# A routed-expert decoder layer: output products by column halves, eleven places for expert weights

## The chip, the core and the metric

The kernel runs on one core of a Trainium2 chip. The core has a matrix engine (TensorE, PE in the rows), VectorE (DVE), ScalarE (ACT), GpSimd (POOL) and SyncE (SP), which run their own streams of instructions and meet by semaphores, and 16 DMA engines, which serve the queues that SP and POOL write. The metric is the device time of one execution in microseconds (us).

## What is computed

One decoder layer on 544 token rows of 1024 values in float32: 512 prompt rows (token tiles 0 to 3 of 128) and 32 decode rows (tile 4). After the attention and pooling branches comes the part that the change touches, cut from the reference:

```
x = x + merged @ w['w_out']
hn = rms_norm(x, w['norm_ffn_g'])
g_prob = softmax(hn @ w_route_group + b_route_group);  g_w, g_idx = top_k(g_prob, 1)
e_logits = (hn @ w_route_expert + b_route_expert)[rows, g_idx]
top_l, top_i = top_k(e_logits, 2);  comb = g_w * softmax(top_l)
expert_block: (silu(xb @ w_gate[e]) * (xb @ w_up[e])) @ w_down[e]
x = x + sum over the two chosen experts of comb * expert_block(hn)
```

There are 32 experts (4 groups of 8). An expert has 1024 x 512 gate and up weights and 512 x 1024 down weights, 6 MB together.

## The kernel before

The kernel is written for each engine by hand, one block an engine, in the order in which the instructions are issued. Nothing is scheduled by a tool. The stages, with the times of the profiled execution:

- up to about 440 us: norms, projections, attention, pooling and the two branch products, ending in `merged` (lines up to 1888);
- 442 to 510 us: the output products. `dec_out` makes those of the decode rows, then `half_out(j, c, part)` makes tile `ORDER[j]`, columns 512c to 512c+511, in two parts of four k-steps each. `ORDER` is 4, 0, 1, 2, 3. A "half" is counted by `half_no(j, c)`, 0 for the decode rows and 1 to 8 for the others: both halves of a tile, then the next tile. Between the parts PE transposes the half before (`turn`, four 128 x 128 transposes, behind the add of x on VectorE, `add_out`), and behind the second part it forms that half's router logits (`route`, w_route with 36 columns). ScalarE squares the sums (`square`), takes the root (`root2`), copies the transposes out of PSUM (`take_turned`) and writes the normalised rows (`normalised`), which go to `hn_rows` in HBM. VectorE chooses the experts of a tile (`choice`), marks each row's rank in its expert's list (`hits`), and PE sums ranks and lists (`tile_ranks`, `tile_list`);
- 510 to 525 us: the last tile's choice, the lists of rows by expert, and the first gathers;
- 525 us to the end: the experts, one step each. `gather_x` on POOL fetches up to 64 rows of `hn_rows` into `x_rows`; PE transposes them (`turn_x`), multiplies by up and gate weights (`gate_up`, whose two parts free two weight places by `ga_used` and `gu_ready`), transposes the hidden rows (`turn_hid`) and multiplies by the down weights (`down`, `dn_ready`); `add_y` adds the result to y in HBM by an indirect DMA.

Expert weights come in 96 chunks of 2 MB (two of up and gate, one of down for each expert) on the SP queue, by `load_chunk(n)`, into place n mod `N_CHUNK` = 10 of `CHUNK_AT` in one big SBUF array, `arena`. Places 0 to 6 are free when the branch products end. Place 7 is the first half of w_out, place 8 its second half, place 9 lies in `merged`. From chunk 10 on each load waits until the chunk ten before it is used (lines 625 to 629). The first nine and what goes between them on SP:

```
            sp.wait_ge(y_start[ORDER[0]], 16)
            sp.wait_ge(turned, 1)
            sp.wait_ge(hn_ready, 1)
            load_x(ORDER[4])
```

The last of these lines loads x of token tile 3 a second time: tile 3 and the decode rows share one place (`x = [x_at[0], x_at[1], x_at[2], x_at[3], x_at[3]]`), so it waits until the decode rows' y is stored and their transposes and hn rows are done. Behind it come the y stores of tiles 0 to 2, chunk 7, the y store of tile 3, its hn rows, chunk 8, and chunk 9 behind `x_full[0]`, the landing of the first gather.

On PE, DVE and ACT the expert steps are a first step, ten written out, a loop of ten that runs twice, and a last one.

## Time and profile before

| | us |
|---|---|
| median of 3 runs | 1030.26 (1027.77 to 1032.42) |
| profiled execution | 1030.08 |
| its span, first to last instruction | 1028.2 |
| TensorE busy | 903.1 (88% of the span) |
| VectorE, ScalarE, GpSimd busy | 365.2, 224.2, 85.4 |
| read from and written to HBM | 252.46 and 14.58 MB |

The page gives the busy shares of the engines and, in 40 slices of 25.7 us, how busy they and the DMA engines are. Since the stages have different limits, the share over the whole span says little: one reads the slices, then the stretch in question, and there which wait ends last. PE's busy time counts pipelined matmuls whose ends are modelled. The clock that TensorE was granted is given with each stretch as a share of full speed, 2.4 GHz; 0.50 is 1.2 GHz.

### The profile page before, as it was taken

How to read it: one execution, taken by the hardware profiler on the slowest of the kernel's cores; microseconds unless marked ns; L12 is line 12 of the kernel's file. 1: busy time of each engine (PE TensorE's matmuls, PEld its weight loads, DVE VectorE, ACT ScalarE, POOL GpSimd, SP SyncE). 2: the span in 40 equal slices, each digit the busy share in tenths (PEclk: the TensorE clock that was granted, in tenths of full speed). 3: DMA queues.
4: the chain of work that ended last, by engine and by line, in shares of the span. 5: the costliest groups of instructions: out<-in, count | busy, mean ns of one | idle time of the engine just before them, and what ended most of it. 6: DMA issues, size and time to landing. Idle time of an engine off the chain costs nothing.

```text
span 1028.2 us, 11181 instructions
## 1 busy us (share of the span) xinstructions
PE 903.1 (88%) x4299; PEld 507.0 (49%) x4299; DVE 365.2 (36%) x806; ACT 224.2 (22%) x570; POOL 85.4 (8%) x88
## 2 busy tenths in 40 slices
PE   6899799999899999999969999797777778887884
PEld 5454577777678888855533333233232323232331
DVE  4588568767343345533334111111011111111110
ACT  3432354254632100022211111001000000000010
POOL 0100000000000000000011211011111111010111
PEclk9999899999999999999969999899999999989998
DMA  9621212111112227088389999999999999999991
GB/s 316 202 82 71 93 42 81 51 42 58 66 42 82 83 82 263 15 346 339 144 301 400 395 388 393 390 411 397 400 401 403 410 398 413 403 413 396 405 393 44
DMA packets 33327, 258.46 MB, mean 251 GB/s; under 512 B 9000, under 2 KB 12328, under 8 KB 17768
## 3 DMA queue, kind: packets, MB, share of 16 engines
q1 hardware_dynamic: 27376, 245.45, 60.0%
q0 software_dynamic: 5904, 12.37, 4.6%
q8 instruction: 30, 0.49, 0.2%
q14 instruction: 17, 0.14, 0.0%
HBM read 252.46 MB, written 14.58 MB: 260 GB/s over the span
## 4 chain that ended last, share of the span: by engine, by line
PE 56%; DMA 26%; DVE 8%; issue 4%; ACT 4%; another core or an unknown queue 1%; SPq 1%; POOL 0%; POOLq 0%; DVEq 0%; ACTq 0%
DMA arena<-in_w_gu 19%; PE ps L1731 19%; PE ps L2004 12%; PE ps L2023 7%; PE ps L1670 6%; PE ps L1888 5%; DMA arena<-in_w_ed 5%; DMA arena<-in_x 2%; PE ps L1993 2%; DVE arena L1297 1%; ACT arena L833 1%; DVE a_stat L1323 1%; DVE arena L1320 1%; ACT arena L845 1%; PE ps L1747 1%
## 5 line engine op out<-in xcount | busy, mean ns | idle before, releaser
L1731 PE MATMUL ps<-arena 128*128 128x272 f32 x1120 | 269.4, 397 | 13.4 <-ACT arena L733 5.8
L2004 PE MATMUL ps<-arena 128*64 128x512 f32 x512 | 235.2, 608 | 20.7 <-DMA arena<-in_w_gu 20.4
L1731 PEld LDWEIGHTS ps<-arena 128*128 128x128 f32 x1120 | 209.9, 191 | 65.0 <-ACT arena L733 11.5
L2005 PE MATMUL ps<-arena 128*64 128x512 f32 x512 | 235.4, 609 | 0.0
L2023 PE MATMUL ps<-arena 128*64 128x512 f32 x512 | 132.9, 666 | 56.6 <-issue 44.0
L733 ACT ACTIVATE arena<-ps 128x272 f32<-128x272 f32 (+5 forms) x172 | 77.3, 457 | 399.0 <-PE ps L2023 172.8
L2004 PEld LDWEIGHTS ps<-arena 128*64 128x64 f32 x512 | 67.5, 139 | 158.9 <-issue 125.5
L1529 DVE SCALAR_TENSOR_TENSOR arena<-ps,list_w,arena 64x512 f32<-64x512 f32 x32 | 23.7, 742 | 290.1 <-ACT arena L998 290.1
L2023 PEld LDWEIGHTS ps<-arena 128*64 128x64 f32 x512 | 43.4, 151 | 143.2 <-issue 134.5
L1670 PE MATMUL ps<-arena 128*128 128x512 f32 (+1 forms) x192 | 75.2, 549 | 8.8 <-DMA arena<-in_w_kv 7.4
L692 POOL DMA_INDIRECT out_y<-arena,list_i x32 | 45.6, 1426 | 403.4 <-PE ps L1993 346.1
L998 ACT ACTIVATE arena<-ps 64x512 f32<-64x512 f32 x32 | 19.0, 594 | 233.8 <-PE ps L2005 233.8
L1536 DVE COPY arena<-ps 64x512 f32<-64x512 f32 x32 | 21.8, 682 | 129.1 <-PE ps L2023 129.1
L2005 PEld LDWEIGHTS ps<-arena 128*64 128x64 f32 x512 | 67.4, 139 | 0.0
L1888 PE MATMUL ps<-arena 128*128 128x512 f32 x128 | 58.5, 599 | 0.0
L1670 PEld LDWEIGHTS ps<-arena 128*128 128x128 f32 x192 | 38.0, 203 | 39.4 <-issue 27.9
L1993 PEld LDWEIGHTS ps<-const,arena 64*128 64x128 f32 x256 | 30.6, 200 | 25.5 <-issue 25.5
L833 ACT ACTIVATE arena<-arena,a_stat 128x256 f32<-128x256 f32 (+1 forms) x64 | 30.0, 470 | 30.7 <-DVE a_stat L1325 30.7
L1993 PE MATMUL ps<-const,arena 64*128 64x64 f32 x256 | 34.8, 279 | 0.5 <-DMA arena<-hn_rows,list_i 0.5
L1888 PEld LDWEIGHTS ps<-arena 128*128 128x128 f32 x128 | 23.0, 190 | 23.6 <-issue 23.4
L686 POOL DMA_INDIRECT arena<-hn_rows,list_i x32 | 30.3, 948 | 42.0 <-DVE list_i L1494 20.5
L683 POOL DMA_DIRECT2D hn_rows<-arena x4 | 2.1, 536 | 316.8 <-ACT arena L972 316.8
(224 smaller groups left out, 691.3 us busy)
## 6 DMA issues: line engine op xcount, KB each, us to landing
arena<-in_w_gu SPq DMA_DIRECT2D x64, 2048.0 KB, 48.7
arena<-in_w_ed SPq DMA_DIRECT2D x32, 2048.0 KB, 50.9
arena<-in_w_pair SPq DMA_DIRECT2D x20, 1024.0 KB, 4.8
arena<-in_x SPq DMA_DIRECT2D x8, 512.0 KB, 8.6
arena<-in_w_q SPq DMA_DIRECT2D x2, 2048.0 KB, 15.4
arena<-in_w_out SPq DMA_DIRECT2D x2, 2048.0 KB, 12.5
arena<-in_x_T SPq DMA_DIRECT2D x4, 512.0 KB, 9.3
out_y<-arena SPq DMA_DIRECT2D x4, 512.0 KB, 5.9
```

The lines of the kernel that those rows point to most:

```text
L686: pool.indirect_dma_start(out=x_rows[s][0:C, :], out_offset=None, in_=hn_rows, in_offset=bass.IndirectOffsetOnAxis(ap=index, axis=0), boun ...
L692: pool.indirect_dma_start(out=o["y"], out_offset=bass.IndirectOffsetOnAxis(ap=index, axis=0), in_=y_rows[s][0:C, :], in_offset=None, compu ...
L733: return act.activation(out, in_, ACT.Copy)
L833: act.activation(p, p, ACT.Exp, bias=a_stat[:, s, 0, c:c + 1], accum_out=a_stat[:, s, 1, c:c + 1])
L1529: stt(hid[s][0:C, :], ps[0:C, 2 + s, :], weight, silu[s][0:C, :], ALU.mult, ALU.mult)\
L1670: ins = mm(ps[0:r, bank, 0:w], hU[:, k, t * P:t * P + r], slot(u, KD, w)[:, k, :], start=k == 0, stop=k == KD - 1)
L1731: ins = mm(out, w[:, k, :], tokens[:, k, :], start=k == 0 and q in "127", stop=k == 3, skip_group_check=q not in "127")
L1888: ins = mm(ps[:, 2 * (j % 2) + c, :], merged[:, k, t * P:(t + 1) * P], w_out[c][:, k, :], start=k == 0, stop=k == KD - 1)
L1993: ins = transpose(ps[:, s, j * C:(j + 1) * C], rows[:, j, :], ident[0:C, 0:C])
L2004: mm(ps[0:C, 2 + s, :], xT[s][:, j, :], w[:, jj, 0, :], start=j == 0, stop=j == JX - 1)
L2005: ins = mm(ps[64:64 + C, 2 + s, :], xT[s][:, j, :], w[:, jj, 1, :], start=j == 0, stop=j == JX - 1)
L2023: ins = mm(ps[64 * q:64 * q + C, 6 + s, :], hidT[s][:, j, :], w_down(n)[:, j, 512 * q:512 * q + 512], start=j == 0, stop=j == JH - 1)
```

## The change

Three parts, as the code has them.

First, the halves are numbered with the first column halves of all four tiles ahead of the second ones (`half_no`, `half_of`), and PE, DVE and ACT walk them in that order. Four PSUM banks take turns. Only one k-step of a half now stands ahead of the transposes of the half before, two more ahead of its router product. A tile's logits come from two halves that lie apart, so the first half's part is made in PSUM columns of its own, copied to SBUF once (`part_logits`) and scaled before the second part is added.

Second, there are eleven places. The new one is where the x tiles were (8192), and place 9 moves by 256 words. To make room, the gathered rows, the y rows, silu and hidden rows of even experts use partitions 0 to 63 and those of odd ones 64 to 127 of the same words, and the scratch of `list_items` lies in the table of constants. On SP chunk 7 comes behind half 4 and ahead of the y stores of tiles 0 to 2, chunk 8 behind half 8, chunk 9 behind the y store of tile 3 with no wait for a gather, chunk 10 behind the landing of all y stores. POOL issues the first gathers without having waited for y stores, and waits for them ahead of the first add to y.

Third, the weights are laid out on the host so that the transposes of gathered and hidden rows read blocks of 128 neighbouring columns and not every eighth or fourth one; each chunk stays 128 rows of 16 KB. PE's expert steps are all written out.

```diff
-N_CHUNK = 10
+N_CHUNK = 11
-        CHUNK_AT = [19584 + 4096 * c for c in range(7)] + [0, 4096, 15232]
+        CHUNK_AT = [19584 + 4096 * c for c in range(7)] + [0, 4096, 15488, 8192]
...
         def half_no(j, c):
-            return 0 if j == 0 else 2 * j - 1 + c
+            return 0 if j == 0 else (NT - 1) * c + j
...
             load_x(ORDER[4])
+            sp.wait_ge(out_ready, half_no(NT - 1, 0) + 1)
+            load_chunk(EARLY)
             for j in range(1, NT - 1):
                 start_y(j)
-            sp.wait_ge(out_ready, half_no(NT - 1, 0) + 1)
-            load_chunk(EARLY)
-            start_y(NT - 1)
+            sp.wait_ge(out_ready, half_no(NT - 1, 1) + 1)
+            load_chunk(EARLY + 1)
             sp.wait_ge(hn_ready, NT)
             t = ORDER[NT - 1]
             sp.dma_start(hn_rows[t * P:t * P + ROWS[t], :], ...).then_inc(hn_last, 16)
-            load_chunk(EARLY + 1)
-            sp.wait_ge(x_full[0], 16)
+            start_y(NT - 1)
             load_chunk(EARLY + 2)
+            for t in range(NT):
+                sp.wait_ge(y_start[t], 16)
+            load_chunk(EARLY + 3)
...
             for j in range(1, NT):
                 add_out(j, 0)
-                choice(j - 1)
                 half_mean(j)
+                if j == 1:
+                    choice(0)
+                if j == 3:
+                    hits(0)
+            for j in range(1, NT):
                 add_out(j, 1)
+                if j == 1:
+                    dve.wait_ge(logit_ready, NT)
+                    dve.tensor_copy(part_logits, ...).then_inc(first_logits, 1)
...
                 inverse2(j)
-                hits(j - 1)
-            choice(NT - 1)
+                if j > 1:
+                    hits(j - 1)
+                choice(j)
             hits(NT - 1)
...
             dec_out()
+            for h in range(1, 2 * NT - 1):
+                half_out(h, (0,))
+                turn(h - 1)
+                half_out(h, (1, 2))
+                if h > NT + 1:
+                    tile_ranks(h - NT - 1)
+                route(h - 1)
+                half_out(h, (3, 4, 5, 6, 7))
...
-                rows = x_rows[s][0:C, :].rearrange("c (p j) -> c j p", j=JX)
+                rows, own = split(x_rows[s], (JX, P)), slice(64 * s, 64 * s + C)
```

How it moves PE's instructions, at the start of the output products. Before (L1888 is `half_out`, L1899 and L1903 `turn`, L1919 `route`, L1930 `tile_ranks`):

```order
L1888 MATMUL ps<-arena 128x512 x4
L1899 MATMUL ps<-const,arena 128x32 x8
L1888 MATMUL ps<-arena 128x512 x4
L1919 MATMUL ps<-arena 32x36 x8
L1888 MATMUL ps<-arena 128x512 x4
L1903 MATMUL ps<-const,arena 128x128 x4
L1888 MATMUL ps<-arena 128x512 x4
```

After, at the same place (L1907 is `half_out`, L1918 and L1923 `turn`, L1943 `route`):

```order
L1907 MATMUL ps<-arena 128x512
L1918 MATMUL ps<-const,arena 128x32 x8
L1907 MATMUL ps<-arena 128x512 x2
L1943 MATMUL ps<-arena 32x36 x8
L1907 MATMUL ps<-arena 128x512 x6
L1923 MATMUL ps<-const,arena 128x128 x4
L1907 MATMUL ps<-arena 128x512 x2
```

The transposes of a half have moved from behind four k-steps of the next one to behind one; the five k-steps that end a half and the first of the next stand together as x6.

On the SP queue, from the second load of x of tile 3 to the first reuse of a chunk place. Before (L591 and L593 are chunks, L599 y stores, L618 the last hn rows):

```order
L582 DMA arena<-in_x 128x1024 [waits hn_ready,turned,y_start4]
L599 DMA out_y<-arena 128x1024 [waits x2_ready] x3
L593 DMA arena<-in_w_ed 128x4096 [waits out_ready]
L599 DMA out_y<-arena 128x1024 [waits x2_ready]
L618 DMA hn_rows<-arena 128x1024 [waits hn_ready]
L591 DMA arena<-in_w_gu 128x4096
L591 DMA arena<-in_w_gu 128x4096 [waits x_full0]
L593 DMA arena<-in_w_ed 128x4096 [waits ga_used]
```

After:

```order
L587 DMA arena<-in_x 128x1024 [waits hn_ready,turned,y_start4]
L598 DMA arena<-in_w_ed 128x4096 [waits out_ready]
L604 DMA out_y<-arena 128x1024 [waits x2_ready] x3
L596 DMA arena<-in_w_gu 128x4096 [waits out_ready]
L624 DMA hn_rows<-arena 128x1024 [waits hn_ready]
L604 DMA out_y<-arena 128x1024 [waits x2_ready]
L596 DMA arena<-in_w_gu 128x4096
L598 DMA arena<-in_w_ed 128x4096 [waits y_start3,y_start2,y_start4,y_start1,y_start0]
L596 DMA arena<-in_w_gu 128x4096 [waits ga_used]
```

Chunk 7 has moved ahead of three y stores, the wait for the gather is gone, and a fourth chunk stands between the last y store and the first reuse.

## Rows read from the trace of the kernel before

**Rows 1.** The page: busy tenths of the DMA engines in 40 slices.
```profile
DMA  9621212111112227088389999999999999999991
```
**Rows 2.** Busy time by stretch; the last three numbers: PE's clock, DMA share, GB/s.
```profile
485.00:510.00 25.00, 25.00 (x90) 13.18 (x89) 9.63 (x46) 5.12 (x11) 0.53 (x1) 1.00 0.33 128
510.00:532.00 22.00, 14.53 (x91) 9.44 (x92) 9.37 (x40) 3.77 (x7) 3.83 (x4) 0.61 0.73 263
...
540.00:600.00 60.00, 60.00 (x304) 24.14 (x302) 17.78 (x39) 7.91 (x16) 9.64 (x9) 1.00 1.01 394
...
900.00:960.00 60.00, 50.51 (x222) 20.23 (x222) 6.75 (x10) 5.70 (x11) 9.49 (x8) 0.89 1.01 408
```
**Rows 3.** Bytes moved from 430 to 600 us, in 40 slices of 4.25 us.
```profile
GB/s 0 2 89 424 428 416 432 432 432 424 432 359 269 5 2 125 154 339 127 175 332 278 203 373 224 432 377 415 432 396 376 394 395 364 416 399 361 424 384 374
```
**Rows 4.** Issues of the SP queue in order: start, us from first to last, line.
```profile
454.65 0.33 SPq L582 DMA_DIRECT2D arena<-in_x  x1
...
501.17 0.34 SPq L593 DMA_DIRECT2D arena<-in_w_ed  x1
...
513.68 0.33 SPq L618 DMA_DIRECT2D hn_rows<-arena  x1
514.05 10.88 SPq L591 DMA_DIRECT2D arena<-in_w_gu  x2
532.64 0.33 SPq L593 DMA_DIRECT2D arena<-in_w_ed  x1
```
**Rows 5.** DMA issues at 454 to 455 and 966 to 967: KB, us to landing.
```profile
arena<-in_x SPq DMA_DIRECT2D x1, 512.0 KB, 28.0
...
arena<-in_w_ed SPq DMA_DIRECT2D x1, 2048.0 KB, 48.4
```
**Rows 6.** Instructions in order of time at the first half product: start, us, engine.
```profile
442.36 3.70 PE L1888 MATMUL ps<-arena 128*128 128x512 f32 x8
...
442.60 1.71 DVE L1407 TENSOR_TENSOR arena<-ps,arena 32x256 f32<-32x256 f32 x4 [1.76 <-PE ps L1878]
...
447.01 0.36 ACT L733 ACTIVATE arena<-ps 128x256 f32<-128x256 f32 x1
```
**Rows 7.** The same view over one half product, number 4.
```profile
467.73 0.26 DVE L1439 SCALAR_TENSOR_TENSOR arena<-ps,stat,r_bias 128x36 f32<-128x36 f32 x1
467.97 3.70 PE L1888 MATMUL ps<-arena 128*128 128x512 f32 x8
...
471.75 0.25 DVE L1459 TENSOR_SCALAR arena<-arena,const 128x64 f32<-128x64 f32 x1
...
475.38 0.98 PE L1919 MATMUL ps<-arena 128*128 128x36 f32 x8
475.65 0.69 DVE L1410 TENSOR_TENSOR arena<-ps,arena 128x512 f32<-128x512 f32 x1 [3.59 <-PE ps L1888]
...
476.44 3.68 PE L1888 MATMUL ps<-arena 128*128 128x512 f32 x8
```
**Rows 8.** The chain that ended last, from 505 to 560 us, at the first gather.
```profile
520.66 3.91 DMA arena<-hn_rows,list_i
...
524.71 2.00 PE ps L1993 x16
```
**Rows 9.** Landing of gathers 3 and 4, gather 5, all 32, and the hn stores.
```profile
DMA to landing us min/median/max: 6.1/6.5/6.8
...
DMA to landing us min/median/max: 9.1/9.1/9.1
...
DMA to landing us min/median/max: 3.1/10.8/11.6
...
DMA to landing us min/median/max: 2.9/3.9/10.3
```
**Rows 10.** The chain that ended last: two pieces of 16 down matmuls.
```profile
814.52 5.35 PE ps L2023 x16
...
1014.52 3.67 PE ps L2023 x16
```

More of the change, by code:

```diff
@@ L699, in _ @@
             pool.wait_ge(hn_last, 16)
-            for t in range(2):
-                pool.wait_ge(y_start[t], 16)
             pool.wait_ge(rows_listed, 1)
@@ L704, in _ @@
                 gather_x(list_i[:, e:e + 1], e)
-            for t in range(2, NT):
-                pool.wait_ge(y_start[t], 16)
             for e in range(2, NE + 4):
@@ L710, in _ @@
                     gather_x(list_i[:, e:e + 1], e % 2)
+                if e == 4:
+                    for t in range(NT):
+                        pool.wait_ge(y_start[t], 16)
                 if e >= 4:
@@ L1012, in step @@
                 take_y(e - 1, 1 - s, half - (1 - s))
-            for t in range(2, NT):
-                act.wait_ge(y_start[t], 16)
             do_silu(0, 0)
@@ L1880, in dec_out, with half_out @@
                 ins.then_inc(out_ready, 1)
-            def half_out(j, c, part):
+            def half_out(h, ks):
+                j, c = half_of(h)
                 t = ORDER[j]
-                if part == 0 and j > 1:
-                    pe.wait_ge(x2_ready, half_no(j - 2, c) + 1)
-                for k in range(4 * part, 4 * part + 4):
-                    ins = mm(ps[:, 2 * (j % 2) + c, :], merged[:, k, t * P:(t + 1) * P], w_out[c][:, k, :],
+                if ks[0] == 0:
+                    above(pe, x2_ready, h - 3)
+                for k in ks:
+                    ins = mm(ps[:, out_bank(h), :], merged[:, k, t * P:(t + 1) * P], w_out[c][:, k, :],
                              start=k == 0, stop=k == KD - 1)
-                if part == 1:
+                if ks[-1] == KD - 1:
                     ins.then_inc(out_ready, 1)
@@ L1913, in route @@
                     pe.wait_ge(x2T_last, 1)
[L1914 removed]
+                j, c = half_of(h)
                 t = ORDER[j]
[L1916 to L1919 removed]
+                above(pe, logits_taken, j if c == 1 else 1)
+                if h >= NT:
+                    pe.wait_ge(first_logits, 1)
+                at = 36 * t if c == 1 else 36 * (NT + t)
+                ks = range(KD) if h == 0 else range(4 * c, 4 * c + 4)
+                for k in ks:
+                    rows = dec_x2T[:, k, :] if h == 0 else x2T[(h - 1) % 2][:, k % 4, :]
+                    ins = mm(ps[0:ROWS[t], 6, at:at + 36], rows, w_route[:, k, :], start=k == ks[0],
+                             stop=k == ks[-1])
                 ins.then_inc(logit_ready, 1)
@@ L2039, in _ @@
             step(0, 0, 0, 0)
-            for k in range(1, 1 + UNROLL):
-                step(k, k, k // 2, 0)
-            with pe.Fori(1, STEPS) as it:
-                for k in range(1, 1 + UNROLL):
-                    step(it * UNROLL + k, k, it * (UNROLL // 2) + k // 2, it * (16 * 3 * UNROLL // N_CHUNK))
+            for e in range(1, NE):
+                step(e, e, e // 2, 0, last=e == NE - 1)
             e = NE - 1
-            step(e, e, e // 2, 0, last=True)
             turn_hid(e, 1)
```

88 lines of the change are left out of this document (42 added, 46 removed).

## The prediction

> **What bounds the kernel now.** I read the page's busy shares and slices first, then the busy times by stretch, then the queue's issues in order of time, and last the start of the expert stage instruction by instruction. TensorE is the busiest engine, but in the second half of the span the 16 DMA engines are busy in every slice [rows 1], and the stretches at 540 to 600 and 900 to 960 us show a DMA share of 1.01 at 394 and 408 GB/s, while PE falls to 50.5 of 60 us [rows 2]. So the expert stage is bound by the 96 chunks of 2 MB. The only loss there is before it: at 485 to 510 us the DMA share is 0.33 and at 510 to 532 it is 0.73 [rows 2], while PE runs the output products without a gap. The end is therefore set by two things: when chunk place 0 is first given back (the load behind `ga_used`, 532.64 us [rows 4]), and how many chunks are still to be loaded then. In the kernel before, chunks 0 to 9 have been issued by then and 86 are left. The last is issued at about 966 us and lands 48.4 us later, at 1014.4 [rows 5]; the last down product, begun at 1014.52 [rows 10], the copy and the add to y end the span at 1028.2. From the first chunk of a reused place to the last landing this is (1014.4 - 532.6) / 86 = 5.6 us a chunk; by the bytes alone, 2.097 MB at 394 to 432 GB/s [rows 2, 3], it is 4.9 to 5.3.
>
> **The gain: one more place.** With eleven places, 85 chunks are left when place 0 comes back. That takes off one chunk, between 4.9 us (bytes at the 432 GB/s of the best slices [rows 3]) and 5.6 us (all traffic included). I take 5.5, nearer to the upper end, since it is the pace at which chunks really landed. Loading chunk 7 at the end of the fourth product, not the seventh (issued at 501.17 now [rows 4]), earns nothing by itself: it has landed long before place 0 comes back in either kernel. Chunk 8 waits for the last product in both, and so is not earlier. The chunk that no longer waits for the first gather (524.6 now, the second of the pair at 514.05 [rows 4]) had landed by 532.6 anyway. So the first reuse of a place (call it T, 532.64) decides: each us that T is late costs one, against 5.5 gained.
>
> **What the new order of the products does to T.** One product (half the columns of a tile) with its transposes and router product takes 8.47 us, from 467.97 to 476.44 [rows 7]; all eight run without a gap. The new order issues the same matmuls; what changes is what lies between an instruction and what it waits for.
> (1) Start. The transposes of the decode tile now stand behind one k-step of the first product (0.86 us, a quarter of 3.44) and not four. The add that they need ends at 442.60 + 1.71 = 444.31, and PE is there at 442.36 + 0.86 = 443.22: 1.1 us of stall. The transposes and two k-steps take it to about 446.7; the router product then waits for the copy by ScalarE, which stands behind its table load and root and ends at 447.37: 0.7 us more [rows 6]. Together +1.8 us.
> (2) The tile whose x shares its place. `load_x(ORDER[4])` fetches token tile 3 into the place of the decode rows, at 454.65, behind chunks 0 to 6, and lands 28.0 us later, at 482.65 [rows 4, 5]. Before, its first use is the seventh product (over at 501), so this was free. Now it is the fourth, over at 442.36 + 1.8 + 4 x 8.47 = 478.0. The add on VectorE waits for the tile, and PE stops after one k-step of the fifth product, at 478.9, until the add is done. The store of tile 0's hn rows (0.5 MB, 1.2 us at that rate) no longer goes before it, since the second halves now come later; so I take a landing of 481.4, an end of the add 0.8 later (0.69 us [rows 7]), and a stall of 3.4 us. Bounds: 2.2 (one y store less in the way as well) and 4.7 (482.65 as measured).
> (3) VectorE's choice of a tile (467.73 to 472.0, 4.3 us [rows 7]) now lies in the second pass between the router product, 4.2 us into a cycle, and the next add. It ends about when the next product does; the k-step covers what is left. I take 0 to 1 us in all, and 0.3 of it under the next point.
> (4) Last product: one router product (0.98 [rows 7]) more and one small list product less stand ahead of its end; I take +0.6, with the 0.3 of (3) inside the rounding. The two ops before the last choice (the scaled half logits) are issued before the wait for the router product, where VectorE is idle anyway.
> The last product thus ends 1.8 + 3.4 + 0.6 = 5.8 us later. From there to the list of rows nothing is shorter or longer.
>
> **What the new order of the queue does to T.** Now the first gather is issued at 520.66 and lands in 3.91 us: chunk 8 has just gone and chunk 9 is held back until the gather has landed [rows 4, 8]. In the new order chunk 8 (at the end of the last product), the hn rows, the y store, chunk 9 and chunk 10 are issued within some 10 us, 7.3 MB or 17 to 19 us of transfer, and the gather falls in their middle. Rows show 6.1 to 6.8 us with one chunk in flight, 9.1 with two and 10.8 as the median of the stage [rows 9]. With chunk 9 going and chunk 10 behind it the row with two is nearest: +5.2 us, with bounds of +2.6 (6.5) and +6.9 (10.8). The store of the last hn rows (513.68 now [rows 4], 5.8 later then) stands behind chunk 8; with one chunk ahead of it it lands some 5 us after its issue, and the gather's own issue comes 7.0 after it, so I cost that at nothing. If it takes the 10.3 us that such a store took under load [rows 9], it costs up to 4.
> The Trainium skill, "DMA: Bandwidth & Descriptors", section "Queues, rings and completion order", says that every DMA engine takes turns between the queues that have work, a packet at a time. By that rule a gather, on another queue than the chunks, would not be slower for the second chunk behind the first. The rows do not agree, since they go from 6.5 to 9.1 and 10.8 us; by the rule the sum would be 2.6 us lower.
>
> **What costs nothing.** The packing of the expert weights keeps the pieces: each chunk is 128 rows of 16 KB in both. The transposes of gathered rows read 128 neighbouring words and not every eighth; even at zero PE time this would not move T by more than part of the 2.0 us that the first two take [rows 8], and I take 0 (-1 at best). PE's loop over experts is written out; PE has some 10 us of 60 idle in the stage [rows 2], and that cover would have to go before it cost anything. Shared silu and hidden buffers wait for what had to be done anyhow.
>
> **The sum.** T: +5.8 + 5.2 = +11.0 us. Chunks: -5.5. Net +5.5 us on the profiled execution's 1030.08 us, which stands within 0.2 of the median 1030.26: **1035.6 us**. The bounds of the terms give 1.8 + 2.2 + 0.6 + 2.6 - 5.6 = +1.6 and 2.0 + 4.7 + 1.4 + 6.9 - 4.9 = +10.1, or 1031.7 to 1040.2.
>
> **Rivals.**
> One or both waits don't come. If tile 3 has landed in time (it shares the queue with less traffic than now), the net is +2.1 and the time 1032.2; if instead the gather is not slowed, +0.3, 1030.4; with neither, 5.5 - 1.8 - 0.6 = 3.1 us are gained, 1027.0. This is not slower, and it is decided at two points: the landing of tile 3 against 478.9, and the gather's landing against 4 us. For it: traffic ahead of both is a matter of a few hundred KB. Against: 28.0 us and 9.1 us are measured.
> Faster: the eleventh place raises the rate of the stage. The stage runs at 394 to 408 GB/s while slices of pure chunk traffic reach 432 [rows 3]; were the lack of issued chunks the reason, even 2% more on 85 chunks of 5.6 us would be worth 9.5 us, and the time 1026 us. Against it: the share is 1.01 with ten places already.
> Worse: the stall at the fifth product drops PE's clock. The same 16 matmuls took 5.35 us in one expert and 3.67 in another [rows 10]; after a stall of 3.4 us one such piece at half the clock adds 1.7 us or more. With the hn store late as well the time is 1038 to 1042 us.
> That the new order does what it says is hardly open: the rows of both orders show it.
>
> **How the numbers follow.** Forecast 0.50, spread over 1032 to 1039; waits missing 0.20, 1027 to 1032; rate up 0.15, below 1026; worse 0.15, 1038 to 1042. The range 1026 to 1041 leaves out most of the rate rival and the end of the last. About 0.5% (5.2 us) is what a measurement can tell from no change. Of the forecast's 0.50 some 0.30 lies above 1035.4 and 0.20 within; with the others: slower 0.30 + 0.15 = 0.45, same 0.20 + 0.20 = 0.40, faster 0.15.
>
> **What would show it.** In the profile after: the load behind `ga_used` at about 543.6 us (right if 540 to 547); one idle time of PE of about 3.4 us ahead of the transposes of tile 3's first half; the first gather's landing in 7 to 11 us; a DMA share near zero for some us before 543; from there 5.5 to 5.6 us a chunk. The forecast is wrong if T moves by less than 6 us, or if the stage's GB/s differ from before by more than 1%.

## The result, and the profile after

| | before | after |
|---|---|---|
| median, us | 1029.28 (1027.77 to 1032.42, 6 runs) | 1038.90 (1037.25 to 1041.40, 6 runs) |
| profiled execution, us | 1030.08 | 1038.97 |
| its span, us | 1028.2 | 1037.1 |
| TensorE busy, us | 903.1 | 891.3 (86% of the span) |
| read and written, MB | 252.46 and 14.58 | 252.45 and 14.58 |

The changed kernel takes 1.0100 times as long as the one before (95% interval 1.0080 to 1.0119): 9.6 us slower in the medians, 8.9 in the profiled spans. The forecast was 1035.6 us, and slower by over 0.5% was its likeliest sign. The profiled executions start the first half product at 442.36 us before and at 442.92 after. No instruction of the change stands ahead of it, so 0.56 us of every later difference in time between the two profiles is not its doing.

The page's line on the DMA engines, and the bytes per slice of 430 to 600 us, both of the kernel after. They answer to [rows 1] and [rows 3]:

```profile
DMA  8522212112112227097378999999999999999992
...
GB/s 0 2 62 393 428 405 432 432 432 432 432 285 401 8 123 123 127 123 123 125 162 333 438 385 348 138 69 58 420 404 373 432 405 376 366 388 387 428 390 369
```

In the second line, slices of 4.25 us, the queue is saturated up to about 485 us, thin while the second column halves are made (123 to 127 GB/s), full for four slices, and thin again (138, 69, 58) in the three slices up to 549 us. Before, that second hole held 203 and 224 GB/s in two slices that do not touch. From there on the engines are as full as before (a share of 1.01; the stretch of 540 to 600 us still holds the end of that hole). The same stretches as in [rows 2], of the kernel after, with PE's granted clock, the DMA share and GB/s at the end:

```profile
485.00:510.00 25.00, 25.00 (x86) 12.18 (x85) 11.42 (x50) 7.58 (x15) 1.09 (x2) 1.00 0.27 109
510.00:532.00 22.00, 12.92 (x80) 8.62 (x79) 13.44 (x63) 5.41 (x9) 2.52 (x3) 0.76 0.75 279
540.00:600.00 60.00, 58.99 (x304) 22.04 (x306) 17.95 (x39) 7.26 (x14) 10.76 (x10) 0.95 0.90 345
900.00:960.00 60.00, 45.68 (x223) 16.48 (x220) 7.60 (x11) 5.30 (x10) 8.97 (x8) 0.97 1.01 402
```

The issues of the SP queue of the kernel after, in order (start, us from first to last, line), answer to [rows 4]:

```profile
455.41 0.33 SPq L587 DMA_DIRECT2D arena<-in_x  x1
478.61 0.33 SPq L598 DMA_DIRECT2D arena<-in_w_ed  x1
490.19 17.82 SPq L604 DMA_DIRECT2D out_y<-arena  x3
515.99 0.34 SPq L596 DMA_DIRECT2D arena<-in_w_gu  x1
519.47 0.32 SPq L624 DMA_DIRECT2D hn_rows<-arena  x1
519.83 0.43 SPq L604 DMA_DIRECT2D out_y<-arena  x1
520.31 0.51 SPq L596 DMA_DIRECT2D arena<-in_w_gu  x1
527.47 0.33 SPq L598 DMA_DIRECT2D arena<-in_w_ed  x1
546.89 3.76 SPq L596 DMA_DIRECT2D arena<-in_w_gu  x2
```

T, the first reuse of a place, is 546.89 us in place of 532.64. From T to the end of the span it is 490.2 us with 85 chunks left; before it was 495.6 with 86.

PE's instructions of the kernel after, with what ended the idle time ahead of them, at the start of the output products, at the tile whose x is loaded late, and at the first expert. They answer to [rows 6 to 8]:

```profile
444.92 0.68 PE L1918 MATMUL ps<-const,arena 32*128 32x32 f32 x8 [0.88 <-DVE arena L1413]
448.06 0.68 PE L1943 MATMUL ps<-arena 128*32 128x36 f32 x16 [0.55 <-ACT arena L740]
481.80 0.66 PE L1923 MATMUL ps<-const,arena 128*128 128x128 f32 x4 [2.37 <-DVE arena L1416]
...
537.36 1.08 PE L2019 MATMUL ps<-const,arena 64*128 64x64 f32 x8 [7.29 <-DMA arena<-hn_rows,list_i]
539.92 1.08 PE L2019 MATMUL ps<-const,arena 64*128 64x64 f32 x8 [1.48 <-DMA arena<-hn_rows,list_i]
```

And the chain of work that ended last, of the kernel after, from the store of the last hn rows to the first expert product:

```profile
519.47 6.76 DMA hn_rows<-arena
...
527.26 1.03 POOL arena L694
...
528.59 11.20 DMA arena<-hn_rows,list_i
539.92 1.08 PE ps L2019 x8
```

Every predicted stall is there, and two more steps (L694 is `gather_x`; the chain goes through the second gather, issued at 528.59): the chain now runs through the hn store (6.76 us), and PE waits 1.48 us for the gather of the second expert before it touches the weights of the first.

### The profile page after: what moved, and what is told of

The parts are those of the page before. It is cut to its first block, busy times and chain, and to the rows that moved or that the text cites. A ratio compares the mean times of both kernels' runs of the same rounds, so it can differ in the third digit from the quotient of the medians.

```text
span 1037.1 us, 11143 instructions
## 1 busy us (share of the span) xinstructions
PE 891.3 (86%) x4299; PEld 488.8 (47%) x4299; DVE 368.4 (36%) x811; ACT 224.1 (22%) x570; POOL 85.6 (8%) x88
## 3 DMA queue, kind: packets, MB, share of 16 engines
HBM read 252.45 MB, written 14.58 MB: 257 GB/s over the span
## 4 chain that ended last, share of the span: by engine, by line
PE 65%; DMA 11%; DVE 8%; issue 8%; ACT 4%; another core or an unknown queue 2%; SPq 1%; POOL 0%; DVEq 0%; POOLq 0%; ACTq 0%
PE ps L2030 20%; PE ps L1749 18%; PE ps L2049 12%; PE ps L1688 6%; DMA arena<-in_x 4%; DMA arena<-in_w_gu 4%; PE ps L1907 2%; PE ps L2019 2%; DVE arena L1303 1%; ACT arena L840 1%; DVE a_stat L1329 1%; DMA arena<-hn_rows,list_i 1%; DVE arena L1326 1%; DMA out_y<-arena 1%
## 5 line engine op out<-in xcount | busy, mean ns | idle before, releaser
L1907 PE MATMUL ps<-arena 128*128 128x512 f32 x128 | 59.4, 602 | 0.0
L2019 PEld LDWEIGHTS ps<-const,arena 64*128 64x128 f32 x256 | 19.0, 143 | 34.5 <-issue 34.5
L694 POOL DMA_INDIRECT arena<-hn_rows,list_i x32 | 30.5, 953 | 44.9 <-issue 24.6
L1907 PEld LDWEIGHTS ps<-arena 128*128 128x128 f32 x128 | 22.7, 190 | 21.6 <-issue 21.5
L2019 PE MATMUL ps<-const,arena 64*128 64x64 f32 x256 | 23.5, 234 | 8.8 <-DMA arena<-hn_rows,list_i 8.8
```

The lines of the kernel that those rows point to most:

```text
L694: pool.indirect_dma_start(out=x_rows[s][0:C, :], out_offset=None, in_=hn_rows, in_offset=bass.IndirectOffsetOnAxis(ap=index, axis=0), boun ...
L1907: ins = mm(ps[:, out_bank(h), :], merged[:, k, t * P:(t + 1) * P], w_out[c][:, k, :], start=k == 0, stop=k == KD - 1)
L2019: ins = transpose(ps[:, s, j * C:(j + 1) * C], rows[:, j, :], ident[own, own])
```

## The experiments

Theory one, with which the experiments began, was the prediction's own ledger: T moves by the stalls, and a place is worth one chunk, 5.5 us. Its rivals were that one of the stalls was not the cause, and that the eleventh place was. After four runs the ledger no longer explained the times, and theory two took its place: **the stage from 560 us on moves bytes at one rate, some 401 GB/s, in every version; the end moves by the bytes that were not moved by then.** Times of single events are compared below as the profiles have them; where runs reached the first half product at different times, the difference counted from there is given beside it.

### The late x tile and the crowded gathers

Run e1 loads x of tile 3 ahead of chunks 5 and 6. Run e2 holds chunks 9 and 10 until both first gathers have landed. Run e3 does both.

```diff
 # e1
-            for n in range(2, EARLY):
+            for n in range(2, 5):
                 load_chunk(n)
...
             load_x(ORDER[4])
+            for n in range(5, EARLY):
+                load_chunk(n)
 # e2
             start_y(NT - 1)
+            for s in range(2):
+                sp.wait_ge(x_full[s], 16)
             load_chunk(EARLY + 2)
```

> The changed kernel, with the second load of x of token tile 3 issued ahead of chunks 5 and 6 instead of behind them. Theory (the end moves by what the first reuse of a chunk place, T, moves; the x tile holds PE up at the fifth product): the idle time of 2.37 us ahead of the transposes of half 4 goes, the last product ends 2.4 us earlier, T falls from 546.9 to 544.5, time 1038.9 - 2.4 = 1036.5 us. Rival (the loss lies in the expert stage itself, in its rate, and not ahead of T): the idle time goes as well but the time stays at 1038.9.

> The changed kernel, with chunks 9 and 10 held back on the queue until the first two gathers have landed. Theory (the first gathers are slow because chunks 8 to 10 are in flight beside them): the first gather lands about 4 us after its issue instead of 10.8, the wait of 1.5 us for the second goes as well, T falls by 8.4 to 538.5 and the time to 1030.5 us. Rival 1 (gathers are slow for another reason: packing into half the partitions, or the queue of POOL): the landing stays over 8 us, and with the chunks later the time is 1038.9 or more. Rival 2 (loading 9 and 10 early was worth their time): T falls but the queue is empty for longer, and the time stays within 2 us of 1038.9.

> Both edits: x of tile 3 ahead of chunks 5 and 6, and chunks 9 and 10 behind the first two gathers. Theory: the two add, T at 536.1 and 1028.1 us, which is before's time less one chunk (5.5) plus the stalls at the start (1.8), the longer stretch before the last product's end and the clock (2 to 3). Rival (only one of the two is on the path): no better than the better of the two alone, 1030.5.

Measured: e1 1033.59 us, ratio 1.0043 (1.0016 to 1.0071); e2 1034.37, 1.0056 (1.0036 to 1.0076); e3 1032.38, 1.0037 (1.0021 to 1.0053). In these and all later runs the kernel before, on the same chip, had medians of 1028.6 to 1029.0. The rows of e1 (waits of PE at the two gathers, first reuse) and then of e2 (the chain's gather, first reuse):

```profile
534.09 1.08 PE L2021 MATMUL ps<-const,arena 64*128 64x64 f32 x8 [7.87 <-DMA arena<-hn_rows,list_i]
536.57 1.09 PE L2021 MATMUL ps<-const,arena 64*128 64x64 f32 x8 [1.40 <-DMA arena<-hn_rows,list_i]
542.64 3.76 SPq L596 DMA_DIRECT2D arena<-in_w_gu  x2
```
```profile
526.78 3.85 DMA arena<-hn_rows,list_i
539.08 3.76 SPq L596 DMA_DIRECT2D arena<-in_w_gu  x2
```

Both causes are shown: in e1 PE's wait at tile 3 is gone and T is 4.3 us earlier (2.8 counted from the first half product); in e2 the gather lands in 3.85 us and T is 7.8 us earlier (7.4). The median of e1 is 2.9 us below what its theory gave, more than the wait explains; its seven times spread over 5 us. But T does not set the price alone. In e2 SP issued nothing from 519.5 to 531.2, the DMA engines had little to do, and only 4.5 of the 7.8 us reached the time. That was the first miss: I expected 1030.5. With both stalls gone e3 has T = 533.96, 1.3 us from the kernel before (3.3 counted from the first half product), and yet nothing of the chunk's 5.5 us: its T to the end is 495.6 us, as with ten places. Its time is above both that it was given (1028.1 and 1030.5).

### The parts alone

Run e4 is the changed kernel with ten places. e6 is the kernel before with the new order of products alone; chunk 7, which waits for a half by its number, goes out earlier with it (475.8 us). e7 is the changed kernel with the old order of products and the old order on SP, with chunk 10 behind chunk 9, both behind the first gather. e11 is the kernel before with the packed weights alone.

```diff
 # e4, against after
-N_CHUNK = 11
+N_CHUNK = 10
...
-            for t in range(NT):
-                sp.wait_ge(y_start[t], 16)
-            load_chunk(EARLY + 3)
 # e7, against after
             load_chunk(EARLY + 1)
+            sp.wait_ge(x_full[0], 16)
             load_chunk(EARLY + 2)
             for t in range(NT):
                 sp.wait_ge(y_start[t], 16)
             load_chunk(EARLY + 3)
 # e11, against before
-                rows = x_rows[s][0:C, :].rearrange("c (p j) -> c j p", j=JX)
+                rows = x_rows[s][0:C, :].rearrange("c (j p) -> c j p", j=JX)
```

> The changed kernel with ten places: chunk 10 is loaded at the first reuse of a place and not ahead of it. Theory (one place is worth one chunk of 5.5 us at the end): T as in the changed kernel or up to 3 us earlier, since one chunk less is beside the first gathers; time 1038.9 + 5.5 - (0 to 3) = 1041.4 to 1044.4 us. Rival (the eleventh chunk only crowds the first gathers and its place brings nothing): 1036 to 1038.9.

> The kernel before with the new order of the output products alone: ten places, chunk 9 behind the first gather as before, old weight layout. Theory: the last product ends 6 us later (stalls of 0.9 and 0.55 us at the start, 2.4 us for x of tile 3, and a router product more ahead of it), the first gather still lands in 4 us, T goes from 532.6 to 538.7, the time from T to the end stays 495.6: span 1034.3, 1036.1 us device time, against 1028.8 before. Rival (the new order costs less than its stalls, since work moves out of the tail behind the last product): T at 536 or less, 1033 us or less.

> The kernel before with eleven places and the new weight layout alone: old order of the products, chunk 9 behind the first gather as before, chunk 10 right behind it. Theory A (what counts is from when on the queue never runs empty, and how many chunks are left then): the queue is full from 524.6 on with 87 chunks left, which took 503.1 us to the end in the run with both edits, so span 1027.7 and 1029.5 us, the same as before. Theory B (the forecast's reckoning: T unmoved, one chunk less to load behind it): 1028.8 - 5.5 = 1023.3 us.

> The kernel before with the third part of the change alone: the weights laid out on the host by column blocks, so that the transposes of gathered and hidden rows read 128 neighbouring words; ten places, the old order of products and PE's loop stay. Theory (packing only shortens transposes that stand beside the bound transfers): T lower by 0 to 1 us, the stage at the same 401 GB/s, time 1028 to 1030. Rival (the layout in HBM or in the arena changes the rate of the chunks): over 2 us off in either direction, with another GB/s at 600 to 1000 us.

Measured: e4 1037.34 us, 1.0085 (1.0056 to 1.0114); e6 1032.93, 1.0060 (1.0038 to 1.0083); e7 1027.84, 0.9999 (0.9983 to 1.0015); e11 1029.61, 0.9998 (0.9986 to 1.0009).

e4 came out where the rival had it. The ledger, with up to 3 us allowed for the gathers, had it 2.5 to 5.5 us slower than the changed kernel; it was 1.6 us faster, which is within what the two intervals leave open. Its rows (first gather in the chain, PE's wait, first reuse):

```profile
526.11 5.67 DMA arena<-hn_rows,list_i
531.92 1.57 PE L2016 MATMUL ps<-const,arena 64*128 64x64 f32 x16 [3.24 <-DMA arena<-hn_rows,list_i]
539.26 0.33 SPq L598 DMA_DIRECT2D arena<-in_w_ed  x1
```

Chunk 10 alone takes the gather from 5.67 us to over 10, and T from 539.26 to 546.89. Counted from the first half product the place costs 6.3 us there (7.6 by the times as they stand) and gives 5.9 back after T (490.2 against 496.1). What e4 contradicts is thus the 3 us allowed for the gathers, not yet the sum of T and chunks left; e3 and e7 contradict that. In e7, where no such price is paid, T is 531.68 and T to the end 495.2 us: the place gave 0.3 us, not 5.5. The queue is hardly empty at that place in the old order: before, chunk 9 was issued at 524.6 and took 8.7 us, so it was still landing at T. An earlier chunk 10 then only makes chunk 11 land later. That is theory two. Here are the bytes moved from 436 to 560 us, first of before, then of after, e4 and e7:

```profile
DMA packets 4000, 37.24 MB, mean 300 GB/s; under 512 B 643, under 2 KB 643, under 8 KB 2086
```
```profile
DMA packets 3681, 33.33 MB, mean 269 GB/s; under 512 B 595, under 2 KB 595, under 8 KB 1995
```
```profile
DMA packets 3760, 34.54 MB, mean 279 GB/s; under 512 B 600, under 2 KB 600, under 8 KB 2000
```
```profile
DMA packets 4086, 37.74 MB, mean 304 GB/s; under 512 B 673, under 2 KB 673, under 8 KB 2150
```

And the stretch of 600 to 1000 us of before, after and e7 (PE's clock, DMA share, GB/s at the end):

```profile
600.00:1000.00 400.00, 326.29 (x1494) 126.53 (x1492) 50.54 (x75) 39.31 (x75) 57.62 (x49) 0.95 1.01 403
```
```profile
600.00:1000.00 400.00, 319.48 (x1516) 114.52 (x1514) 51.82 (x75) 39.26 (x75) 58.37 (x50) 0.94 1.01 402
```
```profile
600.00:1000.00 400.00, 316.90 (x1474) 114.94 (x1472) 51.74 (x75) 39.21 (x75) 56.19 (x47) 0.92 1.01 401
```

(e4's line has the same share of 1.01 with 402 GB/s and is left out; the third line is e7's.) The kernel after had moved 3.91 MB less by 560 us. At 401 GB/s that is 9.8 us; its span is 8.9 longer. The same for all runs, spans against the 1028.2 of before:

| run | MB, 436 to 560 | shortfall / 401 GB/s, us | span, us | difference | first half product, us | difference from there | median, us |
|---|---|---|---|---|---|---|---|
| before | 37.24 | 0 | 1028.2 | 0 | 442.36 | 0 | 1029.28 |
| after | 33.33 | +9.8 | 1037.1 | +8.9 | 442.92 | +8.3 | 1038.90 |
| e13 (below) | 33.94 | +8.2 | 1036.8 | +8.6 | 442.62 | +8.3 | 1037.56 |
| e4 | 34.54 | +6.7 | 1035.4 | +7.2 | 441.60 | +8.0 | 1037.34 |
| e2 | 34.88 | +5.9 | 1034.7 | +6.5 | 442.51 | +6.4 | 1034.37 |
| e1 | 35.15 | +5.2 | 1033.2 | +5.0 | 441.42 | +5.9 | 1033.59 |
| e6 | 35.92 | +3.3 | 1030.7 | +2.5 | 440.10 | +4.8 | 1032.93 |
| e10 (below) | 36.19 | +2.6 | 1032.3 | +4.1 | 442.51 | +4.0 | 1034.19 |
| e3 | 36.81 | +1.1 | 1029.6 | +1.4 | 440.36 | +3.4 | 1032.38 |
| e7 | 37.74 | -1.2 | 1026.9 | -1.3 | 441.79 | -0.7 | 1027.84 |
| e8 (below) | 37.77 | -1.3 | 1026.4 | -1.8 | 442.15 | -1.6 | 1028.50 |
| e9 (below) | 38.15 | -2.3 | 1026.0 | -2.2 | 440.89 | -0.7 | 1027.98 |
| e12 (below) | 38.20 | -2.4 | 1026.1 | -2.1 | 440.08 | +0.2 | 1029.22 |
| e11 | 38.21 | -2.4 | 1025.1 | -3.1 | 439.58 | -0.3 | 1029.61 |

Since all runs move the same bytes in the end, the agreement is partly bookkeeping. What it shows is that nothing else moved: no version changed the rate afterwards by more than 3 GB/s in 403, and one GB/s over 400 us is 1 us, the size of the residuals. Part of the agreement has another source, which lies ahead of the change: the profiled executions reach the first half product between 439.58 and 442.92 us, and one that gets there early has both more bytes by 560 us and a shorter span. e11 has the shortest span of all for this reason, and a median above those of e7, e8 and e9. The column that counts from the first half product takes it out; it agrees with the difference of the medians, each against the kernel before of its own round, within 1.5 us in all 13 runs, where the whole span is off by up to 3.8 (e11). With the bytes counted from there as well, over the same 117.64 us, shortfall and difference again agree within 1.5 us, so theory two stands without that help.

e6 gives the price of the new order of products alone: +4.3 us of median (3.9 to 8.5 by the interval of its ratio). Its theory had expected 1036.1, its rival 1033 or less, and the rival's number came: T is 4.3 us later, counted from the first half product, and not 6.1. Its PE stalls are those of the changed kernel, 0.88 and 0.55 us at the start and this one at tile 3:

```profile
478.61 0.66 PE L1929 MATMUL ps<-const,arena 128*128 128x128 f32 x4 [2.00 <-DVE arena L1421]
```

e7 and e11 put places and packing at nothing measurable. Order (+4.3) and the rest (0) do not add up to +9.6: about 5 us are in the two together, by subtraction that is in the new order on SP, which e7 does not have and e6 has for chunk 7 alone.

### Holding chunk 10 alone

Run e8 takes e1, makes three k-steps (not one) of the first half product ahead of the transposes, and holds only chunk 10 until both gathers have landed. Run e10 has that hold alone.

```diff
 # e8 and e10, against after
             for t in range(NT):
                 sp.wait_ge(y_start[t], 16)
+            for s in range(2):
+                sp.wait_ge(x_full[s], 16)
             load_chunk(EARLY + 3)
 # e8
-                half_out(h, (0,))
+                half_out(h, (0,) if h > 1 else (0, 1, 2))
```

> The changed kernel with x of tile 3 ahead of chunks 5 and 6, three k-steps instead of one ahead of the first transposes, and chunk 10 alone (not 9) held until the first two gathers have landed. Theory: the last product ends 3.8 us earlier than in the changed kernel, the first gather lands in 5 to 6 us beside chunk 9 alone, T at about 534.5 with chunk 10 just landing; from T on 490.2 us as in the changed kernel: span 1024.7, 1026.5 us. Rival (the queue is what counts, it is full from the issue of chunk 9 or 10 on, and holding any chunk gives back what the gather gains): 1029 to 1031 us, as with both chunks held.

> The changed kernel with one line of SP's order changed: chunk 10 alone waits until both first gathers have landed; chunk 9 goes as in the changed kernel. Theory (the end moves by what the DMA engines leave unused before about 560 us; a place is worth its chunk only if its load does not stand beside the first gathers): the gathers land in 5 to 6 us as with ten places, T is 539 to 540.5, chunk 10 fills the queue while PE makes the first products, and 85 chunks are left: span 1029.5 to 1031.5, time 1031 to 1033, that is 4 to 6 us below the ten-place form (1037.34) with nearly the same T. Rival (a place is worth little whenever its load goes out this late, as in the run that held chunks 9 and 10 both): 1034 to 1035, chunk 10 having only moved idle time.

Measured: e8 1028.50 us, 0.9995 (0.9979 to 1.0011); e10 1034.19, 1.0049 (1.0030 to 1.0068). The rows of e8: PE at the start, with no wait ahead of the transposes any more, then at the gather, and the first reuse. Then the first reuse of e10:

```profile
442.15 2.84 PE L1911 MATMUL ps<-arena 128*128 128x512 f32 x6
444.92 0.68 PE L1922 MATMUL ps<-const,arena 32*128 32x32 f32 x8
...
528.86 1.57 PE L2023 MATMUL ps<-const,arena 64*128 64x64 f32 x16 [3.45 <-DMA arena<-hn_rows,list_i]
...
536.25 3.76 SPq L596 DMA_DIRECT2D arena<-in_w_gu  x2
```
```profile
540.14 3.76 SPq L596 DMA_DIRECT2D arena<-in_w_gu  x2
```

One wait on SP takes 4.7 us off the changed kernel's median; T is 6.8 us earlier. The hold, the early x and the start without stalls take off 10.4 in all, and the time of the kernel before is reached, not beaten; 1028.50 lies between the theory (1026.5) and the rival (from 1029). With T 3.6 us later than before and 490.2 us from T to the end, e8 does show a place worth its chunk. The reading that fits is that chunk 10 fills the hole ahead of T, and that making that hole costs what filling it gives back. e10 fell between its two cases: the span (1032.3) is the theory's, the median (1034.19) lies in the rival's band. Against e4, with T nearly the same (540.14 and 539.26, and 97.6 and 97.7 us behind the first half product), the place is worth 3.1 us in spans and in medians, and 4.0 from T to the end, not 5.5.

### The second gather

Run e13 is the changed kernel with PE's transposes for the second expert behind the up and gate products of the first, as they stand for all later experts.

```diff
-                if not last:
+                if not last and e > 0:
                     turn_x(e + 1, 1 - s, (half + 1 + s) * 16)
...
+                if e == 0:
+                    turn_x(e + 1, 1 - s, (half + 1 + s) * 16)
```

> The changed kernel with PE's transposes of the second gather moved from ahead of the first expert's up and gate products to behind them, so that PE no longer waits 1.48 us for the second gather before it uses chunk 0. Theory: T falls by the wait and the 16 transposes, 1.5 to 3.5 us, to 543.4 to 545.4, and the time by as much, less what the queue regains later: 1035.5 to 1037.5. Rival (the second gather's wait was no cause, PE waits elsewhere instead, since the down product or the clock takes it back): T 546 to 547, 1038.5 to 1039.5.

Measured: 1037.56 us, 1.0074 (1.0054 to 1.0094), T 544.24. PE waits 7.08 us for the first gather and for the second not at all:

```profile
537.12 1.09 PE L2019 MATMUL ps<-const,arena 64*128 64x64 f32 x8 [7.08 <-DMA arena<-hn_rows,list_i]
```

T fell by 2.65 us (2.35 counted from the first half product), so the step is shown to hold T back: it was one of the terms that the prediction did not have. What it costs in time is not shown. The median fell by 1.3 us, to just above what the theory gave (1037.5), but the intervals of the two kernels overlap, and the profiled span, counted from the first half product, is the same to 0.1 us.

### Trying for less than both kernels

Run e9 is e8 with six matmuls of constants, which nobody reads, at the three places where PE rests between the last product and the first gather. Run e12 is e7 with the swap of e13, chunk 8 right at the end of the last product, chunk 9 without a wait, only chunk 10 behind the first gather, and five such matmuls.

```diff
 # e12, against e7
+            sp.wait_ge(out_ready, half_no(NT - 1, 1) + 1)
+            load_chunk(EARLY + 1)
             start_y(NT - 1)
...
-            load_chunk(EARLY + 1)
-            sp.wait_ge(x_full[0], 16)
             load_chunk(EARLY + 2)
             for t in range(NT):
                 sp.wait_ge(y_start[t], 16)
+            sp.wait_ge(x_full[0], 16)
             load_chunk(EARLY + 3)
...
+            def keep_busy(n):
+                for _ in range(n):
+                    mm(ps[:, 2, :], ident, const[:, 0:512], start=True, stop=True)
```

> The same as the one before, plus six dummy matmuls (128 x 512, of constants, into a PSUM bank that nobody reads) in the waits of TensorE between the last product and the first expert. Theory: the granted clock stays at 2.4 GHz or comes back earlier, the first part of the first expert's products takes 3.5 us instead of 5.9, T falls by about 2 us and the time by 1 to 2 us. Rival (T is by then set by the queue: chunk 10 is still landing): T falls, the time does not.

> The run with the old order of products and eleven places, with four edits that all aim at unused transfer time before 560 us: chunk 8 is issued at the end of the last product and not behind the last hn rows, chunk 9 waits for no gather, only chunk 10 waits for the first gather, the transposes of the second gather stand behind the first expert's up and gate products, and five matmuls of constants that nobody reads keep TensorE from resting between the last product and the first gather. Theory: bytes moved at 436 to 560 us rise by 0.8 to 1.6 MB over that run's, so the time is 1024 to 1027. Rival (the early chunks crowd hn rows and gather, and what they win before T they lose after it, as in the changed kernel): 1027.5 to 1029.

Measured: e9 1027.98 us, 0.9995 (0.9977 to 1.0013); e12 1029.22, 1.0002 (0.9989 to 1.0016). e9's gain on e8 (0.5 us) is within the spread, so its expectation is not borne out, and neither is its rival's T: counted from the first half product T did not fall (94.2 us in e9, 94.1 in e8), and the first expert's products began at 1.06 us a matmul, at a granted clock of 0.50, in both. In e9 the last four matmuls of constants stand in the chain themselves, from 524.16 us up to the transposes at 527.93. e12 is 0.2 us above the rival's range. The stretch of 500 to 527 us, of e12 and then of e7, says that PE did run faster in it (granted clock 0.91 against 0.75) and more bytes moved (282 against 253 GB/s):

```profile
500.00:527.00 27.00, 20.99 (x101) 11.68 (x100) 12.18 (x58) 6.06 (x11) 1.99 (x2) 0.91 0.78 282
```
```profile
500.00:527.00 27.00, 19.78 (x116) 13.35 (x116) 13.88 (x61) 6.36 (x11) 3.10 (x4) 0.75 0.70 253
```

The chain of e12 says who took it back:

```profile
511.39 7.92 DMA hn_rows<-arena
...
520.35 5.55 DMA arena<-hn_rows,list_i
...
527.96 1.12 PE ps L2007
```

With chunk 8 ahead of it the hn store took 7.92 us (3.0 in e7), and held back a gather that itself took 5.55. First expert product 527.96 against 525.67 in e7, T 533.74 against 531.68. e12 had reached the first half product 1.7 us earlier than e7 (440.08 against 441.79), so from there it lost 4.0 us to the first expert product and 3.8 to T. Before 560 us it moved 0.46 MB more than e7, not the 0.8 to 1.6 that I expected, and over the same 117.64 us from the first half product 0.31 MB less. The constants did not keep the clock either: PE stood still for 3.60 us ahead of the first gather's transposes, and the first expert's products ran at 0.50 as in e7. No version beat the kernel before by more than a measurement can tell.

## Why the prediction was right, and where it was not

The sign, the mechanism and the sum of the terms up to the last product held; the tail was sized too small. The time came nearer than the change did: the forecast was +5.5 us on one profiled execution of 1030.08, and the medians of six give +9.6 on 1029.28, so 0.8 us of the nearness is the base, by luck. Against the prediction's steps:

- **The stage is bound by chunk transfers, and the end follows T and the chunks left.** Held as an account of this pair: T +14.25, T to end -5.4, sum +8.9.
- **Start, +1.8.** Measured 0.88 + 0.55 = 1.4 us.
- **Late x tile, +3.4, bounds 2.2 to 4.7.** Measured 2.37, near the lower bound: PE was there at 479.4 us and not 478.9, and the add was over at about 481.7 and not 482.2. e1 removes it.
- **Choices and last product, +0.6.** The product ends at 515.96 (509.81 before), 6.15 us later, of which 0.56 lie ahead of the change: 5.6 against 5.8 predicted. With 1.4 and 2.4 measured for the first two terms, 1.8 is left for this one. So one term was three times its size and two were too large, and they cancelled.
- **hn store, at nothing, up to 4.** It took 6.76 us and is in the chain; the gather's issue is 6.6 us later and the product's end 6.1, so I put 0.5 us on it.
- **First gather, +5.2, bounds 2.6 to 6.9.** This is the term that was mis-sized. PE's first transposes come 10.1 us behind the issue (4.05 before), +6.05. I had taken the row with two chunks in flight (9.1); the chain's second gather took 11.20, above the stage's median. Inside the bounds, but the case was heavier than the row. Chunk 8 had landed at 524.7, 2.6 us ahead of the gather's issue; chunk 9 had some 5.6 us to go and chunk 10 was issued 0.2 us behind the gather, so that the whole of it ran beside chunks.
- **Not in the sum at all: the second gather.** `turn_x(1)` stands ahead of `gate_up(0)`. Before, both gathers had landed by 524.7 and it cost nothing; after, PE waits 1.48 us for it. From first transposes to T: 9.53 us against 7.93, +1.6. The sum is 6.6 + 6.05 + 1.6 = 14.25, against the 11.0 predicted. The 3.25 between them are 1.6 for the second gather, 0.85 for the first, 0.5 for the hn store, -0.2 for the product and 0.56 from ahead of the change; it is nearly the whole error of the forecast (3.3 us of 1038.9).
- **The place, -5.5.** The number was right for this pair (5.4) and the rule behind it wrong, so it was luck. Taken as a property of the place it fails in e7 (0.3 us from T to the end, at most 1.3 of span) and e10 (3.1 us). The step said that chunk 9, issued at 524.6, had landed by 532.6; it took 8.7 us and landed at 533.3, so the queue was still at work at T and had no room to give. These runs fit a place that pays its chunk only where the queue would else stand empty. The changed kernel had that hole only since its own T was late. Had the change been forecast by unmoved bytes, the question would have been where the queue is empty, and -5.5 would not have been a term.
- **Packing at nothing.** Held: e11, 0.9998.
- **T itself.** 546.89, just inside the 540 to 547 that was called right.
- **Rival "rate goes up":** fell; 402 against 403 GB/s in 600 to 1000 us. (The forecast called itself wrong if the stage's GB/s differed by more than 1%; 900 to 960 us differ by 1.5%, 402 against 408, but 400 us by 0.2%.) **Rival "one wait is missing":** fell, both came. **Rival "clock drops at tile 3":** PE's products behind the stall ran at the same pace (two k-steps, four matmuls, in 1.88 us, granted clock 1.00), so its mechanism fell too, while its range of time (1038 to 1042) is where the kernel came out, by the longer gathers.

The prediction set the packet-by-packet turns of the Trainium skill ("DMA: Bandwidth & Descriptors", "Queues, rings and completion order") against the rows, and took from them that a second chunk behind the first would not slow a gather. That conclusion fell: the first gather took 3.85 us with no chunk issued beside it (e2), 5.67 beside chunk 9 (e4) and over 10 with chunk 10 issued 0.2 us behind it (after). The turns themselves are not refuted. The landings of chunks 9 and 10 of the kernel after, and of chunk 9 of e4 (last number, us from issue):

```profile
arena<-in_w_gu SPq DMA_DIRECT2D x1, 2048.0 KB, 12.6
arena<-in_w_ed SPq DMA_DIRECT2D x1, 2048.0 KB, 12.1
```
```profile
arena<-in_w_gu SPq DMA_DIRECT2D x1, 2048.0 KB, 12.5
```

In e4 chunk 9, issued at 518.9, was over at about 531.4, and the gather landed at 531.8. In the kernel after chunk 9 was over at about 532.9 with the gather still under way, chunk 10 ran until 539.6, and the gathers landed at 537.3 and 539.8. The first chunk ended before the gather did, so by the turns as well the next chunk would have slowed it. The runs do not tell this from a cost of depth as such; no run has a chunk that outlasts the gather, with and without another behind it.

**What stays open.** e8 is 3.9 us below e3 in the medians, for an earlier chunk 9 and a start without stalls. The pair e10 and e2, which differ in the hold of chunk 9 alone, puts 0.2 us in the medians and 2.4 in the spans on the first, and the stalls at the start are 1.4 us; how the 3.9 divide is not shown beyond that. What the second gather costs in time is open (e13). Nor was the place tried with a gather that reads rows from SBUF and not from HBM.

## What to carry to other kernels

Where a stage is bound by transfers at a fixed rate, price a change by the bytes that the queue fails to move before the stage is saturated, not by the time of one event, count them from a common start (the profiles here differ by up to 3.3 us ahead of the change), and credit one more buffer only with time in which the queue would be empty. Before bulk loads are issued earlier, list the small transfers that the next dependent step waits for (a store, a gather) and keep the bulk behind them: one held chunk of 2 MB was worth 4.7 us here. When a wait grows, look at every sibling of it that stands between the new arrival and the event that counts; here a second gather that had always been free kept PE waiting 1.5 us.

## What the runs showed of the chip

- **A small gather takes three times as long beside bulk loads.** The first gather of 64 rows took 3.5 to 3.9 us with no chunk beside it (e2, e3) or with only the last 1 to 2.3 us of one (before, e6, e7, e11), 5.6 to 6.3 with one of 2 MB under way (e4, e8, e10, e12), and 9.8 to 10.4 with two (after, e1, e13; the second gather there up to 11.6). The store of 0.5 MB of hn rows went from 2.9 to 3.5 us (before, e6, e7, e11) to 6.6 to 7.9 behind one chunk.
- **Strided against contiguous reads of the moving and the loaded tile.** The same 256 transposes of gathered rows, of before and then of e11, by line and form (busy, mean ns):

```profile
L1993 PE MATMUL ps<-const,arena 64*128 64x64 f32 x256 | 34.8, 279 | 0.5 <-DMA arena<-hn_rows,list_i 0.5
L1993 PEld LDWEIGHTS ps<-const,arena 64*128 64x128 f32 x256 | 30.6, 200 | 25.5 <-issue 25.5
```
```profile
L1993 PE MATMUL ps<-const,arena 64*128 64x64 f32 x256 | 23.2, 234 | 0.0
L1993 PEld LDWEIGHTS ps<-const,arena 64*128 64x128 f32 x256 | 18.9, 143 | 25.4 <-issue 25.3
```

  Every eighth word against neighbouring words: a weight load of 200 ns against 143. It is 12 us less of busy time, of the matmuls and of the loads each, on an engine that is not the bound, and no time.
- **TensorE's clock behind a rest.** PE rested before the first gather, and the first five pairs of matmuls of the first expert's products in the kernel after took 1.06 to 1.11 us each, those from the seventh on 0.59; the granted clock was 0.50 up to 545 us and 1.00 from 546, that is 1.2 and then 2.4 GHz. Matmuls of constants raised the granted clock of 500 to 527 us to 0.91 (e12), and the twenty list products took 1.69 us in place of 2.75. They did not carry it to the experts: in e12 it fell to 0.50 while PE waited for the gather, in e9 it had fallen by 520 us, in spite of six matmuls at 513.67 to 516.51, and the first expert's products started at 1.06 us a matmul in both.
